# The second group of four modulation slabs goes through the third ring slot, and is multiplied between the gate projection and the first convolutions

## The reference, cut to what matters

```python
def modulation(cvec, lw):
    m = jax.nn.silu(cvec) @ lw["ada_w"] + lw["ada_b"]
    return jnp.split(m[..., None, :], 6, axis=-1)

def context_layer(x, c_ctx, lw):
    sh1, sc1, g1, sh2, sc2, g2 = modulation(c_ctx, lw)
    h = modulate(rms_norm(x, lw["norm1_g"]), sh1, sc1)
    zq, zk, zv, zqkv, zg, zb, za = jnp.split(h @ lw["w_in"], SPLITS, axis=-1)
    ...
    x = x + g1 * (o_mix @ lw["w_out"])
    x = x + g2 * hier_moe(modulate(rms_norm(x, lw["norm2_g"]), sh2, sc2), lw)
```

## Time and profile before

| | |
|---|---|
| median of three runs | 1236.32 us (1232.29 to 1238.28) |
| profiled execution | span 1231.4 us, first to last instruction; its own time is not listed apart from the runs |
| PE busy | 1099.9 us, 89% of the span |
| DVE, ACT, POOL busy | 560.3, 290.8, 94.4 us |
| HBM read | 314.38 MB |

### The profile page before, as it was taken

The page is one execution under the profiler, slowest core; times in us unless marked ns, Lnnn a source line. Parts: engine busy times, 40 slices in busy tenths (PEclk is TensorE's granted clock), DMA queues, the critical chain, the costliest instruction groups (busy, mean ns, idle before and its releaser), DMA issues.

```text
span 1231.4 us, 18736 instructions
## 1 busy us (share of the span) xinstructions
PE 1099.9 (89%) x7505; PEld 539.0 (44%) x7505; DVE 560.3 (45%) x1436; ACT 290.8 (24%) x717; POOL 94.4 (8%) x112
## 2 busy tenths in 40 slices
PE   4899999698998999987689999987999999997776
PEld 1455544365456333322235655445755733332222
DVE  1257887457248321111262679856744742111124
ACT  0247412233113111000011682232332311100000
POOL 0020001310001000000011000040000100000001
PEclk9899999799999999999989999988999999999988
DMA  8570133886954999999993203356495499999996
GB/s 357 200 194 1 69 94 114 233 327 232 387 200 184 414 423 420 420 422 422 419 363 114 82 1 94 137 132 251 156 377 225 156 414 423 420 420 422 420 422 262
DMA packets 90794, 333.29 MB, mean 271 GB/s; under 512 B 29631, under 2 KB 32071, under 8 KB 59975
## 3 DMA queue, kind: packets, MB, share of 16 engines
q1 hardware_dynamic: 80999, 299.66, 62.5%
q0 software_dynamic: 7392, 23.93, 5.7%
q10 hardware_dynamic: 2304, 8.39, 1.7%
HBM read 314.38 MB, written 17.56 MB: 270 GB/s over the span
## 4 chain that ended last, share of the span: by engine, by line
PE 70%; SPq 10%; DMA 9%; DVE 5%; issue 3%; ACT 2%; DVEq 0%; ACTq 0%
PE bank L576 66%; SPq L1313 10%; DMA arena<-in_moe_w_dram 4%; PE bank L579 4%; DMA ring<-in_w_in_dram 2%; ACT arena L1492 2%; DMA ring<-in_ada_w_dram 1%; DVE x L1822 1%; DMA ring<-in_w_out_dram 1%; DVE ring L1822 1%; DVE x L1814 1%; DVE arena L1814 1%; DVE small L1822 0%; DVE small L2136 0%; SPq L1402 0%
## 5 line engine op out<-in xcount | busy, mean ns | idle before, releaser
L576 PE MATMUL bank<-ring,arena 128*32 128x512 f32 (+1 forms) x2272 | 331.7, 587 | 30.2 <-issue 16.0
L576 PE MATMUL bank<-arena 128*32 128x512 f32 (+3 forms) x1600 | 270.5, 567 | 18.7 <-DMA arena<-in_moe_w_dram 11.0
L1492 ACT ACTIVATE arena<-bank 128x512 f32<-128x512 f32 (+3 forms) x302 | 129.0, 473 | 584.2 <-PE bank L579 400.0
L576 PE MATMUL bank<-ring,hT 128*128 128x512 f32 x576 | 258.2, 604 | 7.8 <-DMA ring<-in_w_in_dram 4.2
L576 PEld LDWEIGHTS bank<-ring,arena 128*32 128x32 f32 (+1 forms) x2272 | 99.3, 114 | 220.7 <-issue 218.3
L576 PEld LDWEIGHTS bank<-ring,hT 128*128 128x128 f32 x576 | 109.6, 194 | 136.7 <-issue 129.6
L1814 DVE TENSOR_TENSOR arena<-bank,mrow 128x512 f32<-128x512 f32 x36 | 24.9, 692 | 229.2 <-PE bank L576 229.2
L576 PE MATMUL bank<-hT,ring 128*128 128x384 f32 x384 | 128.2, 488 | 0.1
L576 PEld LDWEIGHTS bank<-arena 128*32 128x32 f32 (+2 forms) x1600 | 81.5, 124 | 96.7 <-issue 82.4
L576 PEld LDWEIGHTS bank<-hT,ring 128*128 128x128 f32 x384 | 71.2, 190 | 46.9 <-issue 1.3
L579 PE MATMUL bank<-const,arena 128*128 128x128 f32 x443 | 67.1, 287 | 19.5 <-DMA x<-in_x_prompt_dram 8.6
(11 more groups left out here) (157 smaller groups left out, 846.2 us busy)
## 6 DMA issues: line engine op xcount, KB each, us to landing
ring<-in_moe_w_dram SPq DMA_DIRECT2D x120, 1024.0 KB, 20.7
arena<-in_moe_w_dram SPq DMA_DIRECT2D x72, 1024.0 KB, 19.5
ring<-in_ada_w_dram SPq DMA_DIRECT2D x24, 2048.0 KB, 8.8
ring<-in_w_in_dram SPq DMA_DIRECT2D x14, 2048.0 KB, 9.1
ring<-in_w_out_dram SPq DMA_DIRECT2D x4, 2048.0 KB, 9.4
expert_dram<-arena ACTq DMA_DIRECT2D x16, 512.0 KB, 8.3
tok_dram<-arena POOLq DMA_DIRECT2D x6, 512.0 KB, 2.9
arena<-in_na_rpb_dram SPq DMA_DIRECT2D x16, 96.0 KB, 7.0
```

What stands on the lines that cost most here:

```text
L576: return nc.tensor.matmul(out, lhsT, rhs, start=start, stop=stop)
L1492: return nc.scalar.activation(out, in_, func, **kw)
```

## The change

The second group of a layer's `ada` slabs (4 to 7) leaves the mixing. Each of its slabs is loaded into slot 2 (`MIDDLE_SLOT`), one after the other, and the four products stand behind tile 1 of the gate projection, behind `ba_part`, and behind the convolution projections 1 and 3; its columns are made behind projection 6. `mixing_plan` spreads what is left, 8 slabs in layer 0 and 4 in layer 1. The load of slab 4 in layer 1 waits for `x_ready`.

```diff
@@ pre_slabs
-        ada = [("ada", l, i) for i in range(EARLY, N_ADA)]
-        if l + 1 < DEPTH:
-            ada += [("ada", l + 1, i) for i in range(EARLY)]
         first = [("ada", 0, i) for i in range(EARLY)] if l == 0 else []
-        out.append(first + [("win", l, j) for j in WIN_ORDER] + ada + [("wout", l, j) for j in range(N_OUT)])
+        front = []
+        for n, j in enumerate(WIN_ORDER):
+            front.append(("win", l, j))
+            if 0 < n <= SHARE:
+                front.append(("ada", l, EARLY + n - 1))
+        out.append(first + front + mixing_slabs(l) + [("wout", l, j) for j in range(N_OUT)])
     return out
+def mixing_slabs(l):
+    return [("ada", l, i) for i in range(EARLY + SHARE, N_ADA)] + [("ada", l + 1, i) for i in range(EARLY) if l + 1 < DEPTH]
@@ tensor engine
                     slab_job["win", l, 6] = ("act", jobs["act"])
+                    if t == 1:
+                        ada_product(("ada", l, EARLY))
@@
                 last.then_inc(for_dve, 1)
+                ada_product(("ada", l, EARLY + 1))
@@ convolution projections
+                    if f in (1, 3):
+                        ada_product(("ada", l, EARLY + 2 + f // 2))
+                    if f == 6:
+                        ada_cols(("ada", l, EARLY + SHARE - 1))
@@ sync engine
                     elif l:
                         sp.wait_ge(es["y_full"], 3 * BATCHES * l)
+                        if pre_slot[name] == MIDDLE_SLOT:
+                            sp.wait_ge(x_ready, 2 * TILES * l)
                     load_slab(name)
@@ scalar engine
+                    if c == 5:
+                        act.wait_ge(ada_full, slab_job["ada", l, EARLY + SHARE - 1][1])
@@ vector engine
                     if c == 4:
                         gate_sums()
+                        ada_row(("ada", l, EARLY + SHARE - 1))
+                    if c == 6:
+                        ada_col(("ada", l, EARLY + SHARE - 1))
```

More of the change, by code:

```diff
@@ L35 @@
 EARLY = 4
+SHARE = 4
+MIDDLE_SLOT = 2
 PRE_SLOTS = 5
@@ L61 @@
 RULE_AT = 3
-SHARE = 4
 BLOCK = 32
@@ L507, in program, with place_of @@
         pre_slot, pre_turn, held = {}, {}, [0] * PRE_SLOTS
[L509 to L515, removed]
+        def place_of(l, i):
+            kind, layer, j = name = PRE[l][i]
+            late = mixing_slabs(l) + [("wout", l, n) for n in range(N_OUT)]
+            if name in late:
+                return LATE_SLOTS[late.index(name) % 2]
+            if kind == "win":
+                return WIN_SLOTS[WIN_ORDER.index(j)]
+            return j if j < EARLY else MIDDLE_SLOT
         def held_before(slabs, i):
@@ L520, in held_before @@
             return earlier[-1] if earlier else None
-        for slabs in PRE:
+        for l, slabs in enumerate(PRE):
             for i, name in enumerate(slabs):
-                pre_slot[name] = place_of(slabs, i)
+                pre_slot[name] = place_of(l, i)
                 held[pre_slot[name]] += 1
@@ L628, in _ @@
             for l in range(DEPTH):
-                mixing = [name for name in PRE[l][EARLY if l == 0 else 0:] if name[0] == "ada"]
+                mixing = mixing_slabs(l)
                 plan = mixing_plan(mixing)
@@ L1367, in load_slab @@
                     sp.dma_start(dst, src).then_inc(slab_in[pre_slot[name]] if done is None else done, 16)
-                first_mixing = [i for i, name in enumerate(PRE[l]) if name[0] == "ada" and i >= N_WIN][0]
+                first_mixing = PRE[l].index(mixing_slabs(l)[0])
                 for i, name in enumerate(PRE[l]):
@@ L1918, in _ @@
                 mod = mods[:, l]
-                plan = mixing_plan([name for name in PRE[l][EARLY if l == 0 else 0:] if name[0] == "ada"])
+                plan = mixing_plan(mixing_slabs(l))
                 def point(p):
```

## The result

The changed kernel takes 1258.47 us (median of four runs, 1254.39 to 1260.9), the kernel before 1237.3 us beside it (four runs, 1232.29 to 1241.07). The ratio is 1.0175, 95% interval 1.0142 to 1.0209: 1.75% slower. The forecast was 1256.3 us, 1.6% slower, range 1247 to 1263. The profiled execution took 1254.39 us with a span of 1252.6 us, 21.2 us above the span of before; its mean granted clock is 0.955, that of before 0.964.

What follows compares the result with a forecast made beforehand. PE was taken to bound the stage before the mixing, with layer 0's mixing waiting for slab loads. Layer 0 (+8.5 +12.3 +2.1 -15.8) and layer 1 (+8.5 +8.0 +2.1 -5.7) add +20.0 us to 1236.3: 1256.3 us, range 1247 to 1263.

Steps and rivals of the forecast that it cites:

- The wait for slab 6 in layer 0: Behind convolution projection 1, PE idles 12.3 us because slab 6 is issued behind the bias and small DMAs.
- The wait in layer 1: In front of layer 1's mixing, PE idles 8.0 us for slab 6, issued behind the bias DMAs.
- The clock: After each wait for slab 6, PE's matmuls run at a lower clock, adding 2.1 us per layer.
- Slabs 4, 5 and 7: In front of the mixing, these slabs land in time: no wait, with 0 to 0.5 us possible for slab 5.
- Layer 0's mixing: With 8 slabs instead of 12 it becomes like layer 1's mixing before: -15.8 us, bounds 14.0 to 17.0.
- Layer 1's mixing: Losing four products and one set of columns gives back 5.7 us, bounds 0 and 8.5.
- Steps 2 and 3: In layer 1's mixing, dropping these steps' products comes back in full, 2 x 1.9 us.
- step 5: In layer 1's mixing, DVE sets this step's pace, so dropping its product and columns gives only 0.4 us.
- step 7: In layer 1's mixing, the softmax chain alone takes about 5.7 us, so dropping the product gives 1.0 us.
- Slab 6 in time in both layers: Rival: SP passes the small DMAs quickly, so both waits and clock losses vanish; -4.5 us, 1231.8 us, chance 0.08.
- Only layer 0 waits: Rival: slab 6 lands in time in layer 1, removing its wait and clock loss; 1246.2 us, chance 0.06.
- Nothing back in layer 1: Rival: the chain of softmax and rule paces all steps of layer 1's mixing; 1262.0 us, chance 0.08.

Runs made afterwards that it cites:

- Experiment 1: Changed kernel with the eight bias DMAs per layer and layer 0's nine small DMAs issued behind slab 7; 1234.76 us, ratio 0.9976 to the kernel before.
- Experiment 3: Changed kernel with only layer 0's nine small DMAs moved behind slab 6, bias DMAs staying ahead; 1255.84 us, ratio 1.0158 to the kernel before.
- experiment 4: Changed kernel with the products of slabs 6 and 7 two convolution projections later, queue order kept; 1238.64 us, ratio 1.0009 to the kernel before.
- experiment 5: Changed kernel with convolution projection 1 computed three times in layer 0, twice in layer 1, filling the wait; 1268.04 us, ratio 1.0218.
- experiment 7: Changed kernel with the change made in layer 1 alone, layer 0 in its old order; 1254.44 us, ratio 1.0103 to the kernel before.
- experiment 9: Changed kernel with the change in layer 1 alone and, there, the bias DMAs behind slab 7; 1241.62 us, ratio 1.0023 to the kernel before.
- experiment 10: Kernel before with bias DMAs (both layers) and nine small DMAs (layer 0) issued behind `win` 0 instead of `win` 5; 1237.5 us, ratio 0.9998.
- experiment 2: Changed kernel with bias and small DMAs issued behind slab 6, ahead of slab 7; 1251.41 us, ratio 1.0107 to the kernel before.
- experiment 8: Changed kernel with the change in layer 0 alone and, there, bias and small DMAs behind slab 7; 1232.63 us, ratio 0.9946.
- experiment 11: Repeat of Experiment 1: changed kernel, both layers, bias and small DMAs behind slab 7; 1236.91 us, ratio 0.9981 to the kernel before.
- experiment 12: Repeat of experiment 8: change in layer 0 alone, bias and small DMAs behind slab 7; 1234.74 us, ratio 0.9970 to the kernel before.

## Why the prediction was right, point by point

**The wait for slab 6 in layer 0: right.** 12.52 us (predicted 12.3), from an issue at 83.76 (83.2) and a landing of 7.9 us (8.1). Experiment 1 shows the cause. Seventeen small DMAs held the queue for 18.4 us. The rule of the Trainium skill weighed there, that initiating a DMA is usually small relative to the DMA itself (DMA: Bandwidth & Descriptors, section Issuing engines are not separate DMA queues), is about one DMA, and the trace does not contradict it one by one: a bias DMA held the queue for 1.3 us and landed in 7.0. What counted here is the sum over all that stands ahead in the queue. The prediction's "the trace disagrees" set the sum of seventeen issues against one landing, and its "second rival below" is the first of the list.

**The wait in layer 1: right place, too small.** 9.65 us instead of 8.0. The issue at 686.35 is the predicted one (680.1, and layer 1 begins 662.27 - 656.15 = 6.1 us later); the landing took 12.4 us where I had carried 10.8 over from the load that stood there before. Experiment 3 shows the same size, 12.1 us, for slab 6 of layer 0 when it too leaves right behind the bias DMAs. All six loads of slab 6 that leave there (changed kernel, experiments 3, 4, 5 and 7) took 11.3 to 12.7 us, so 10.8 was low.

**The clock: right mechanism, 1.7 us instead of 2.1** in each layer, shown by the window at 0.50 and by experiment 5.

**Slabs 4, 5 and 7: right**, no wait in either layer. Slab 5 left at 57.91 and 667.79 and landed 7.5 us later, which is just in time: a slower landing would have shown. Slab 7 left at 95.44 and not at 93, since the prediction did not carry its own term for the clock into that issue; it had no effect.

**Layer 0's mixing: -16.4 us, predicted -15.8; the agreement is partly luck.** Layer 1's mixing before was the right model of what it becomes, 98.9 against 99.5 us. What it was is the weak side: the prediction took the 115.3 us of one trace, and the same order took 111.7, 111.9 and 113.4 us in experiments 9, 7 and 10. Against their mean with it, 113.1, the gain is 13.6 us.

**Layer 1's mixing: -7.0 us, predicted -5.7; two of its steps were wrong and their errors opposed each other.** Steps 2 and 3 gave 1.8 and 1.9 us, as said. For step 5 I took DVE as the pace and allowed 0.4 us, since DVE had waited only 0.21 us for the scores. Measured from scores to scores on PE, it gave 2.8, of which step 6 took 0.5 back. Two views of DVE: before the change, where the maxima of step 6 start; and in the changed kernel, the two operations up to the start of step 5's maxima:

```profile
893.73 0.43 DVE L1814 TENSOR_TENSOR bank<-bank,arena 128x256 f32<-128x256 f32 x1 [3.11 <-PE bank L576]
```

```profile
903.89 0.69 DVE L1836 TENSOR_TENSOR arena<-arena 128x512 f32<-128x512 f32 x1
904.50 0.42 DVE L1836 TENSOR_TENSOR bank<-bank,arena 128x256 f32<-128x256 f32 x1
```

PE's scores stand at 901.18 in PE's timeline, and the maxima on DVE start at 904.50, behind other operations of DVE's own, with no idle time. So DVE does pace its own work at that point. From maxima to maxima, step 5 took 882.29 - 869.18 = 13.1 us before and 904.50 - 891.78 = 12.7 in the changed kernel: the 0.4 us that I had allowed. What failed is the step from there to PE. PE has work of its own behind the scores, and before the change DVE waited 3.11 us for PE in step 6 (893.73). That slack took up DVE's lateness: from maxima to maxima step 6 fell from 11.4 to 914.03 - 904.50 = 9.5 us, and DVE's wait to 1.21 us. An engine that is late at one instruction sets the pace only if it is still late when PE needs its result. For step 7 I allowed 1.0 us, and it gave 0.1, because two waits came up where the product had stood:

```profile
907.54 3.98 PE L587 MATMUL bank<-ring 128*128 128x128 f32 x32 [0.80 <-DVE ring L1844]
...
917.86 0.85 PE L590 MATMUL bank<-const,arena 128*128 128x128 f32 x6 [1.04 <-DVE arena L1840]
919.80 0.92 PE L587 MATMUL bank<-arena 64*128 64x384 f32 x4 [1.10 <-ACT arena L1512]
```

The first of these rows belongs to step 6. At 917.86 PE waits 1.04 us for DVE and at 919.80 1.10 us for ACT. This is the chain of the softmax, longer than the 5.7 us that I had read from step 8, because step 7 has other work in it: on DVE two operations that take 1.27 us together (915.90), between the maxima and the division, and on ACT eight operations on 128x128 tiles (916.65 to 919.10), behind which the copy that PE waits for starts at 919.20. Step 8 has neither. The last step gave 1.1 us where I had allowed 0.5. These causes are read from the rows; no experiment took them apart.

**The sum.** The measured terms come to 19.5 us where 20.0 were predicted. The span grew by 21.2. The remaining 1.7 us lie in the experts' stages, which I let move as a whole (-0.3 and +2.0 us). The kernel's time differs by more than that between executions (below), so they are no part of the change that can be shown. Each of the two mixings is also off by its single trace: with the means of the table they give back 13.6 and 6.9 us, and the sum becomes +22 us. The forecast holds either way; that its sum agreed with the first pair of traces to half a microsecond is luck.

**The rivals.** Slab 6 in time in both layers, 1231.8 us on paper, did not happen in the changed kernel; experiment 1 is that rival made true, 1234.76 us. Its premise, that issue times are back pressure, is true in part: the eight bias DMAs held the queue for 15.2 us in layer 0 of experiment 10, right behind two slabs, and for 9.2 us in experiment 1. Only layer 0 waits: refuted by the wait of 9.65 us and experiment 7. Nothing back in layer 1: refuted by the 7.0 us.

## What to carry to other kernels

A load that is put into an in-order queue leaves when everything between its place and its slot's release has been issued: add up those issue times row by row, small DMAs first, and compare with the time the load is due. Issue times grow when slabs are in flight, so take them from a place with the same neighbours. Then ask of the stage it came from whether loads pace it; work that leaves a stage bound by loads comes back in full and more (13.6 us for 8.5 in the mean), work that leaves a stage paced by a chain of several engines does not (6.9 for 8.5). So make such a move only in the layer that waits for loads, and bring the queue into the order of the due times with it.

## What the runs showed of the hardware

**A slab's landing depends on its neighbours.** 2 MB from `ada_w` landed in 7.3 to 8.0 us when no other slab or bias DMA was on its way before it (slabs 5 and 7 of the changed kernel). It took 11.3 to 12.7 us right behind the eight bias DMAs, 10.9 to 12.7 when `win` 5 had left 3.2 us before and no bias DMA stood between (slab 6 of experiments 1, 2, 8, 9, 11 and 12), and 14.3 and 15.5 right behind another slab (experiment 2).

**A DMA's issue time depends on what is in flight.** The eight bias DMAs held the queue for 8.9 to 11.6 us in most places, for 11.6 and 13.2 behind two slabs that had left 3 us apart (experiment 2), and for 15.2 and 16.5 behind two that had left together (experiment 10).

**The price of an idle PE.** Before slabs 6 and 7, behind waits of 4.75 us and more the product took 3.62 to 3.64 us in all these traces; behind 2.87 us it took 2.74, behind 2.64 us and less 1.92. But the length of the wait does not settle it. The fourth product of group 0 stands behind a wait of 3.04 to 3.06 us in all fourteen traces, with the same work ahead of it, and took 1.92 us in two of them (before and changed) and 2.37 to 3.64 us in the other twelve. The changed kernel and experiment 4:

```profile
28.32 1.92 PE L587 MATMUL bank<-ring,silu_w 128*32 128x512 f32 x16 [3.05 <-DMA ring<-in_ada_w_dram]
```

```profile
28.34 3.64 PE L587 MATMUL bank<-ring,silu_w 128*32 128x512 f32 x16 [3.05 <-DMA ring<-in_ada_w_dram]
```

The granted clock was 1.00 in the first (28.3 to 30.3 us) and 0.50 in the second (28.3 to 32.0 us). So a wait of 3 us cost anything from nothing to 1.7 us, from one execution to the next.

**One kernel's time goes with its mean granted clock.** Over the 34 executions of the kernel before beside experiments 9 to 12 the time ran from 1229.39 us (clock 0.964) to 1252.19 us (0.946), with a correlation of -0.84, about 9 us for 0.01 of clock; without the two longest it is -0.83 and 8 us. Which of the two is the cause is not shown: a kernel that waits longer also has a lower clock behind its waits. The spread is more than experiments 8 and 12 gain, and it is why they needed a dozen runs each.
